# Folding twelve more gate and up pairs into seven half-products each, with their token sums on VectorE

## The reference, cut to what matters

```python
x = LN1(alpha*x + 0.5*SwiGLU_1(x))
x = LN2(alpha*x + W_mix_out[conv_group(x) | dsa_group(x)])
x = LN3(alpha*x + MemCrossAttn(x, mem))
x = LN4(alpha*x + 0.5*SwiGLU_2(x))

def _swiglu(x, w_gate, w_up, w_down):
    return (jax.nn.silu(x @ w_gate) * (x @ w_up)) @ w_down

mem_k = (mem_prompt @ w_mem_k[l]).reshape(b_p, N_MEM, MEM_HEADS, MEM_HEAD_DIM)
mem_v = (mem_prompt @ w_mem_v[l]).reshape(b_p, N_MEM, MEM_HEADS, MEM_HEAD_DIM)
```

## Time and profile before

| what | us |
|---|---|
| three runs | 2497.05, 2498.04, 2502.54 (median 2498.04) |
| the profiled execution | 2500.18 |
| its span | 2498.3 |
| TensorE busy (matmuls) | 2403.2 |
| VectorE, ScalarE, GpSimd busy | 1236.4, 1080.1, 1299.6 |

### The profile page before, as it was taken

How to read it: one execution, slowest core, us unless ns; L and a number is a source line. 1 busy time by engine, 2 the same in 40 slices (tenths; PEclk the granted TensorE clock), 3 DMA queues, 4 the chain that set the end, 5 groups by cost and what they waited for, 6 DMA issues and landing times.

```text
span 2498.3 us, 40575 instructions
## 1 busy us (share of the span) xinstructions
PE 2403.2 (96%) x15879; PEld 2175.5 (87%) x15879; DVE 1236.4 (49%) x2223; ACT 1080.1 (43%) x2025; POOL 1299.6 (52%) x860
## 2 busy tenths in 40 slices
PE   8999999999999999998999999999989999999998
PEld 8888889888999999987789888888659899899998
DVE  1000002366757566287452689997263436565433
ACT  4333333444545443445543533323463535545341
POOL 4777665543546465422252676766403426556463
PEclk9999999999999999999999999999899999999999
DMA  4444532454233332533121234333502212343322
GB/s 144 122 120 115 162 97 78 137 161 146 79 108 93 93 115 82 156 118 128 34 79 40 69 101 102 110 101 89 171 11 77 60 43 77 112 140 89 116 85 70
DMA packets 427685, 251.85 MB, mean 101 GB/s; under 512 B 23232, under 2 KB 415552, under 8 KB 426224
## 3 DMA queue, kind: packets, MB, share of 16 engines
q1 hardware_dynamic: 389712, 197.88, 27.7%
q10 hardware_dynamic: 35216, 39.38, 4.9%
q0 software_dynamic: 2576, 12.07, 1.3%
HBM read 222.20 MB, written 25.15 MB: 99 GB/s over the span
## 4 chain that ended last, share of the span: by engine, by line
PE 81%; ACT 5%; DVE 5%; POOL 4%; issue 2%; DMA 1%; ACTq 0%; DVEq 0%; POOLq 0%
PE LIN L1052 59%; PE LIN L972 14%; POOL WL L2618 2%; PE TR L1397 1%; PE LIN L1129 1%; ACT WH L1449 1%; POOL XL L2701 1%; PE TR L1105 1%; PE LIN L1345 1%; ACT PR L1995 1%; ACT PT L2020 1%; PE TR L1206 1%; PE TR L1384 1%; DVE SC L2213 1%; DVE PR L2557 1%
## 5 line engine op out<-in xcount | busy, mean ns | idle before, releaser
L2618 POOL TENSOR_TENSOR WL<-WRAW,WH 128x1024 fp32r<-128x1024 f32 (+2 forms) x306 | 715.7, 2344 | 424.6 <-ACT WH L1449 420.5
L1052 PE MATMUL LIN<-XH,WH 128*128 128x256 f32 (+4 forms) x1880 | 601.9, 336 | 21.1 <-DVE Y L2295 6.4
L1052 PE MATMUL LIN<-XL,WH 128*128 128x256 f32 (+4 forms) x1880 | 595.1, 332 | 0.0
L1052 PE MATMUL LIN<-XH,WL 128*128 128x256 f32 (+4 forms) x1880 | 594.6, 332 | 0.0
L1052 PE MATMUL LIN<-HH,WH 128*128 128x256 f32 (+2 forms) x1632 | 465.0, 307 | 1.3 <-POOL HL L2644 0.7
L1052 PE MATMUL LIN<-HL,WH 128*128 128x256 f32 (+2 forms) x1632 | 462.2, 305 | 0.0
L1052 PE MATMUL LIN<-HH,WL 128*128 128x256 f32 (+2 forms) x1632 | 461.4, 305 | 0.0
L1052 PEld LDWEIGHTS LIN<-XH,WH 128*128 128x128 f32 (+1 forms) x1880 | 346.6, 190 | 61.6 <-issue 18.4
L1449 ACT ACTIVATE WH<-WRAW 128x1024 fp32r<-128x1024 f32 (+1 forms) x310 | 318.2, 1028 | 155.6 <-DMA WRAW<-in_ffn_down 52.8
L1052 PEld LDWEIGHTS LIN<-XL,WH 128*128 128x128 f32 (+1 forms) x1880 | 345.8, 189 | 34.1
L1052 PEld LDWEIGHTS LIN<-XH,WL 128*128 128x128 f32 (+1 forms) x1880 | 344.8, 189 | 33.8
(11 more groups left out here) (259 smaller groups left out, 4048.7 us busy)
## 6 DMA issues: line engine op xcount, KB each, us to landing
WRAW<-in_ffn_gate SPq DMA_DIRECT2D x70, 512.0 KB, 3.8
WRAW<-in_ffn_up SPq DMA_DIRECT2D x70, 512.0 KB, 3.8
WRAW<-in_ffn_down SPq DMA_DIRECT2D x64, 512.0 KB, 3.7
WRAW<-in_w_mix_in SPq DMA_DIRECT2D x44, 512.0 KB, 3.8
WRAW<-in_ffn_down SPq DMA_DIRECT2D x32, 384.0 KB, 3.4
WRAW<-in_w_mix_out SPq DMA_DIRECT2D x16, 512.0 KB, 3.7
WRAW<-in_w_mem_q SPq DMA_DIRECT2D x16, 512.0 KB, 3.8
WRAW<-in_w_mem_o SPq DMA_DIRECT2D x16, 512.0 KB, 3.7
```

The source lines that it names most:

```text
L1052: last = pe.matmul(LIN[0:pr.rows, pr.slot, out:out + w], wt[:, SLOT[pr.tile], c, 0:pr.rows], x[:, c, col:col + w], start=(c == 0 and wt is ...
L2618: pool.tensor_tensor(WL[:, SLOT[n], 0:nk, 0:width], raw(n)[:, 0:nk, 0:width], WH[:, SLOT[n], 0:nk, 0:width].bitcast(F32), ALU.subtract).th ...
```

## The change

Group 0's first feed-forward is folded too, in its second and third part: `FOLDED` has (1, 0). Its first part stays plain, and so do the first four products of the second part and the last four tiles of the third; between them stand six pairs in each part, pairs 0 to 5 and 6 to 11. The 16 memory products all go into the first part: one behind each of its whole gate and up products, two behind every fourth, and one behind each down product until none is left.

Group 0's residual has been added to by then, so its token sums can't be made from `Y`. They are made from `XH` and `XL` in ten steps of VectorE (`sums_of_parts`), five for each two sums, each of 4 x 256 elements and waiting for the one before. The keys of the memory are stored away as soon as they are made (`keep` 4), the values after their turn (`keep` 5); the cached values are loaded later and needn't be kept. The memory's cached keys are loaded behind the last pair of group 0.

At the heads of group 1's runs the token sums come one or two places later: behind VectorE's weight sums for the same product, the second two behind the third plain product. In every pair VectorE's second weight sum moves behind the evaluation of the fifth half-product. `scale` goes: the first eight down products of group 1's second feed-forward are now taken by VectorE alone, which multiplies `Y` by alpha and adds the product in one operation.

```diff
-FOLDED = [(1, 1), (2, 1)]
+FOLDED = [(1, 0), (1, 1), (2, 1)]
...
-            if between and not halves and whole % 2 == 0:
+            for _ in range(guests(whole) if between and not halves else 0):
...
+            if folded(which, g) and between and split:
+                ups = self.stage("ffn", g, tiles, KD, lambda k: k < RING, between, (0, 1), lambda whole: 1 + (whole % 4 == 0), which=which,
+                                 after_norm=after_norm)
+            elif folded(which, g):
+                plain = RING if split or (which, g.index, part) == (1, 0, 1) else 0
...
-    ffn[RING].mid.append(("fold sums", which, 0))
-    ffn[RING].end.append(("fold sums", which, 1))
-    for k in range(4):
-        ffn[RING + k].end.append(("fold part", which, k))
+    ffn[RING].end.append(("fold sums", which, 0))
+    ffn[RING + 1].end.append(("fold part", which, 0))
+    ffn[RING + 2].end.extend([("fold sums", which, 1), ("fold part", which, 1)])
+    ffn[RING + 3].end.extend([("fold part", which, 2), ("fold part", which, 3)])
...
+            ffn[turned[KD - 1] + 3].end.append(("keep", 4))
+            ffn[turned[-1] + 2].end.append(("keep", 5))
+            ffn[run[0] - 4].end.append(("fold sums", 1, 0))
+            ffn[run[0] - 3].end.extend([("fold sums", 1, 1), ("fold part", 1, 0)])
+            ffn[run[0] - 2].end.extend([("fold part", 1, 1), ("memory stored",)])
+            ffn[run[0] - 1].end.extend([("fold part", 1, 2), ("fold part", 1, 3)])
+            ffn[run[-1] + 1].mid.append(("memory cache",))
...
-            for k in range(KD // 2):
-                ffn[2 * RING + k].end.append(("scale", k))
...
+def scaled_late(pr):
+
+    return pr.which == 2 and folded(2, pr.g) and pr.part == 0
...
                 if on:
                     sum_weights(following, 1)
-                    sum_weights(following, 2)
                 dve.wait_ge(part_done, 7 * q + 5)
                 dve.scalar_tensor_tensor(FG[:, 1, w:2 * w], chain_bank(two, w), 0.5, PB[:, 0:w], ALU.mult, ALU.add)\
                     .then_inc(part_summed, 1)
                 if on:
+                    sum_weights(following, 2)
                     sum_weights(following, 3)
...
+                if not second:
+                    step(0, XH[:, top, left].bitcast(F32), XH, top, right, ALU.subtract)
+                    step(0, None, XL, top, right, ALU.add)
+                    step(0, None, XL, top, left, ALU.subtract)
+                    step(1, TF[:, 0, :, 0:w], XH, bottom, right, ALU.subtract)
+                    step(1, None, XL, bottom, right, ALU.add)
+                else:
+                    step(2, XH[:, top, right].bitcast(F32), XH, bottom, right, ALU.subtract)
+                    step(2, None, XL, bottom, right, ALU.add)
+                    step(2, None, XL, top, right, ALU.subtract)
+                    step(3, TF[:, 1, :, 0:w], XH, bottom, left, ALU.subtract)
+                    step(3, None, XL, bottom, left, ALU.add)
+                dve.wait_ge(fold_step, 5 * second + 5)
+                dve.drain().then_inc(fold_summed, 2)
...
+                elif pr.kind == "down" and pr.half is None and scaled_late(pr):
+                    y = Y[:, pr.j, cols(pr)]
+                    dve.wait_ge(product, pr.p + 1)
+                    dve.scalar_tensor_tensor(y, y, ALPHA, in_psum(pr), ALU.mult, ALU.add).then_inc(product_read[pr.slot], 1)
```

More of the change, by code:

```diff
@@ L206, in add, with stage @@
         return pr
-    def stage(self, name, g, tiles, nk, blocks, between=(), order=(0, 1), **facts):
+    def stage(self, name, g, tiles, nk, blocks, between=(), order=(0, 1), guests=lambda whole: whole % 2 == 0, **facts):
         made, k, whole = [], 0, 0
@@ L228, in stage @@
                 made.append(self.add(len(self.weights) - 1, "memkv", j, None, None, KD))
+                if not between:
+                    break
         return made
@@ L377, in front @@
         mix[14].end.append(("spill queries",))
-        if not g.sample and folded(1, g1):
-            for i in range(7):
+        if not g.sample:
+            for i in range(4):
                 mix[len(mix) - 8 + i].mid.append(("keep", i))
```

144 lines of the change are left out of this document (87 added, 57 removed).

## The result

The changed kernel takes 2508.11 us (median of nine runs, 2504.89 to 2511.77) where the kernel before takes 2498.86 beside it (nine runs, 2497.05 to 2502.54). The ratio is 1.0035, with a 95% interval of 1.0026 to 1.0044: by the ratio 8.8 us slower, where 5.3 us faster was forecast. The profiled execution took 2510.89 us, its span 2509.1, so against the one of before (span 2498.3) it shows 10.8 us to explain.

A forecast was written before the change was run, and what follows sets the result against it. Matmuls were taken as the bound, TensorE busy 96%. Pairs -12.5, group 0's head +10.5, its second run's end +1.7, group 1's heads -2.8 and -2.2 sum to -5.3: 2498.04 becomes 2492.7 us, range 2484.5 to 2500.5.

The forecast's parts named there:

- The supply of the first part: Group 0's denser first part: weight tiles keep up with TensorE thanks to 4 to 5 us of lead; costs nothing.
- rival D: First part: stores stretch landings from 3.8 to 5.3 us, so weights come late; +10 us, 2503; chance 0.07.
- The landing of the second raw tile: Head of group 0's first run: tile lands about 9.0 us after the first plain product starts (bounds 7.6 and 11).
- The pairs' pitch: Group 0's twelve pairs take 10.1 us each in place of 11.14 for plain gate and up; gain 12.5 us.
- Rival C: Pairs of 256 columns stay at 10.7 us, bound by VectorE's and ScalarE's chain; 6 us come back, 2499; chance 0.17.
- The head itself: Group 0's first run: tokens' low part ready 32.5 us after the first of four plain products starts; +10.5 us together.
- the second wait of 1.1 us: Group 0's head: the next half-product waits for two weight lows and one token low; 1.1 us more.
- the clock: Group 0's head: the clock falls after an idle stretch, making matmuls slower; 0.6 us.
- The lock between VectorE and GpSimd: Group 0's head: five GpSimd operations hold up VectorE's chain; 6.0 us taken, up to 6.5.
- Group 1's heads: Group 1's first runs: -2.8 us in the first feed-forward; -2.2 in the second, from +0.2 at pair 0 and -2.4 behind.
- the replay: Second feed-forward's head in group 1: replaying rows in the new order, pair 0 loses 3.9 us, 3.7 before.
- The scaling: Group 1's second feed-forward: ScalarE no longer scales the residual, sparing three pairs 0.8 us each; -2.4 us.

The follow-up runs named there:

- e10: Changed kernel with two memory products behind each whole gate and up product, memory values' turn and MV stores kept at the changed kernel's place; 1.0024 of the kernel before.
- e1: Changed kernel with VectorE's second weight sum back ahead of the fifth half-product in each pair; 1.0031 of the kernel before, 2503.75 us.
- e3: Changed kernel with both sets of token sums at group 0's head one place earlier in VectorE's queue; 1.0029 of the kernel before, 2504.35 us.
- e4: Changed kernel with the old places of the token sums at group 1's two heads; 1.0028 of the kernel before, 2504.12 us.
- e7: Changed kernel with ScalarE's last high part of a pair's weights made behind the next pair's first copy PA; 1.0012 of the kernel before, 2502.02 us.
- e2: Changed kernel with two memory products behind each whole gate and up product, none among the down products; 1.0009 of the kernel before, 2499.65 us.
- e5: Changed kernel with memory products only behind gate and up products, group 0's token sums and parts during the first part's down products; 0.9981 of the kernel before.
- e9: Changed kernel with memory products spread, group 0's token sums early, ScalarE's last high part behind the next PA; 0.9962 of the kernel before, 2488.81 us.
- e8: Changed kernel with memory products spread, token sums early, ScalarE's last high part late, VectorE's second weight sum back; 0.9972 of the kernel before, 2493.24 us.

## Why the prediction was wrong

**The supply of the first part: the step that failed.** The prediction set a down product and a memory product, 7.04 us, against a buffer's turn of 7.15, found a deficit of 0.1 to 0.3 us for each of six against 4 to 5 us of lead, and called it "nothing, up to 3 if the lead is gone", with rival D at 0.07. It cost 4.1 us in the first part and, by e10 against the changed kernel, 3.3 more at the head, where it makes the tile late. Two things were wrong. The turn of 7.15 was one reading with a landing of 3.55 us in it (912.99, before); the same loop in the changed kernel is 1.07 + 2.40 + 4.0 us and the gaps, 7.6 (124.46 to 132.04). And the lead was counted to the tile's use. It was there (the tile wanted at 122.34 was split by 117.4), but TensorE waits for an eviction that stands in ScalarE's queue behind the conversion of a landing tile, some 4 us ahead of that tile's use, and one landing of 7.04 us was more than this left.

Two long landings, 7.0 and 5.4 us, stand ahead of 2.8 of the 4.1 us, ordinary ones ahead of the other 1.3. D had the mechanism: stores beside a tile, and a turn longer than TensorE's work. Its condition, 4.6 us sustained, was wrong, since single landings did it. That the keys' store stretches the 7.04 is argued and not shown by a run that moves it alone. But all five traces with this order of the first part (the changed kernel, e1, e3, e4, e7) have 6.5 to 7.7 us there. Why the other tile took 5.4 is open; with 5.7 (e1) and 5.1 (e7) there the stand stays, and with 3.8 (e4) it is gone.

**The landing of the second raw tile.** Taken as 4.4 us after its issue, measured 8.7. The prediction named the two stores beside it and gave them next to nothing. With the two tiles of the next pair 3 MB are in flight. e10 gives the stores' share, 3.0 us at the head. The bound of +11 for the landing was also too low: the tile was used at +14.9.

**The pairs' pitch.** 10.1 was taken because TensorE could go at it, and e7 shows that it can: 10.10. Rival C (0.17) named what happened in the changed kernel, VectorE's and ScalarE's chain from one pair to the next, with 3.6 of the 6 us that it set. The room of 0.5 us was worked out from the low part of the weights, and the room of 1.6 us from VectorE's busy time; what ran out was another loop, through ScalarE's queue to `PA`, that the prediction did not follow. The term should have been -8.9.

**The head itself.** The mechanism was right, once its two causes of lateness are away: e2 shows +30.8 for 32.5, and 9.7 us for 10.5. That the sum came so near is in part luck. The low part came 1.7 us sooner, the second wait of 1.1 us did not come, and the clock cost 2.4 us behind the stand and not 0.6. The lock between VectorE and GpSimd stood in the sum with 6.0 us; the lengthened operations add up to 4.6. In the changed kernel four of the ten steps take 2.2 us and the low part 1.95, not 1.2, each when GpSimd is at work:

```profile
204.08 2.22 POOL L2697 TENSOR_TENSOR WL<-WRAW,WH 128x512 fp32r<-128x512 f32 x1 [7.08 <-ACT WH L1484]
206.26 2.24 POOL L2811 TENSOR_TENSOR FP<-FG 128x512 f32<-128x512 f32 x1
...
205.21 2.17 DVE L2246 TENSOR_TENSOR TF<-XH,TF 128x1024 f32<-128x1024 f32 x1
207.42 2.17 DVE L2244 TENSOR_TENSOR TF<-TF,XL 128x1024 f32<-128x1024 f32 x1
```

Each engine's operations are longer for the other's. The Trainium skill (SBUF — State Buffer, "SBUF: two separate sides") states that such two operations lock each other out for a whole instruction, and these rows agree: a step of 1.24 us takes 2.17 beside them. The rule made this term better: without the lock the forecast was +26.5, with it +32.5, and e2 has +30.8.

**Group 1's heads.** In the first feed-forward ScalarE reached `PA` 5.3 us after the pair's start, forecast 5.5. The pair took 14.91 us and not 13.4, and the 1.5 over are slower matmuls: the two half-products behind the stand take 4.60 us at a granted clock of 0.64, where they took 3.11 before. In the second the replay said 3.9 us lost and it was 6.1: the order made the stand 3.45 us where it was 3.01, the second half-product waited 0.53, and the matmuls behind the stand were slower. With faster ones and the same stand e7 loses 4.6. The scaling gave back 2.35 us, as forecast (2.4).

**The range.** It ended at 2500.5. The three misses, 4.1, 5.5 and 3.6 us, have the same sign, and were held apart as rivals of which only one would come.

## What to carry to other kernels

Where a transfer, a split and a conversion turn a buffer, add them up as a loop and set it against TensorE's work per tile. A distance read between two splits elsewhere has the landing of that place in it; ask what else is in flight here. And count the lead up to the first thing that stands in a queue behind the wait for the tile, here an eviction, and not up to the tile's use. When pairs, or anything that repeats, get shorter, follow every engine's queue once around the loop, also through the copies that seem cheap: the bound was one conversion of 0.52 us that stood ahead of a copy. Work that doesn't depend on a late tile belongs ahead of the wait for it in its queue: here (e5 against e2) that alone was worth 8.9 us at pair 0.

## What the hardware showed

The same stand can cost its length or almost double. In the second feed-forward e7 and e9 have the same instructions, and TensorE stands 3.46 and 3.47 us for the same copy. The next three half-products (36 matmuls of 272 columns) took 4.62 us in e7 and 7.40 in e9. The rows are stretches (us, busy by engine, then the granted clock, DMA share and GB/s), first e7, then e9:

```profile
2132.33:2136.95 4.62, 4.62 (x36) 4.62 (x37) 4.48 (x6) 1.15 (x3) 1.51 (x1) 1.00 0.40 117
```

```profile
2122.72:2130.12 7.40, 7.40 (x37) 7.40 (x37) 4.28 (x6) 1.16 (x3) 1.27 (x1) 0.58 0.25 73
```

A granted clock of 0.58 is mostly the lower of the two levels, 1.2 in place of 2.4 GHz. At the head of group 0 the two half-products behind the 6.03 us took 5.26 us at 0.50, the lower level throughout. So a stand of 3.5 us cost up to 2.8 us above its length here. Behind the 2.6 us stands of the first feed-forward the next two half-products were 1.4 to 1.5 us longer than before in every trace that has them. A comparison of two single traces at such a place is worth no more than that. In e1, e5 and e8 stands of 3.46 and 3.47 us went unpunished as e7's did; why is open.

Also unexpected: GpSimd's work was stretched as much as VectorE's (3.35 for 2.40 us), so moving VectorE's steps to where VectorE is idle moved their cost into GpSimd's queue, where 1.7 us of it showed.
